# Feed-forward stage: another order of the additions that free banks, of the weight low parts, and another point at which a weight buffer is given back

## Chip, cores and metric

The kernel runs on one core of one Trainium2 chip. The metric is the device time of one execution, in microseconds (us). Before the change the median of 3 runs is 2047.44 us (2047.1 to 2047.58).

## What is computed

The reference is one step of a two-layer streaming encoder over 512 prompt tokens and 128 sample tokens (640 together), model width 1024. Each layer has an attention or recurrence part, a cross-attention, and then the gated feed-forward part that this change is about:

```python
def conv_ffn(h, prev, w_gate, w_up, conv_w, conv_b, w_down):
    g = h @ w_gate                                   # 1024 x 2816
    gp = jnp.concatenate([prev.astype(g.dtype), g], axis=1)
    c = conv_b
    for j in range(CONV_W):                          # 3 taps along the tokens
        c = c + conv_w[j] * gp[:, j:j + t]
    y = (jax.nn.gelu(c) * (h @ w_up)) @ w_down       # 2816 x 1024
    return y, gp[:, t:]
```

All of it is float32. The kernel reaches that accuracy by writing each operand as a high and a low part and taking three products: high by high, high by low, low by high.

## The kernel before, in words

**The stage.** `FFN_PLAN` (L117) lists the chunks of one layer: gate/up chunks `gu 0` to `gu 10`, each of 256 columns of gate and of up, and down chunks `dn 0` to `dn 5`. The order is gu 0, gu 1, dn 0; gu 2, gu 3, dn 1; gu 4, gu 5, dn 2; gu 6, gu 7, dn 3; gu 8, gu 9, gu 10, dn 4, dn 5. In this text a *pair* is one of the six groups gu 2/3, gu 4/5 and gu 6/7 of the two layers with their dn; the *triple* is gu 8/9/10; the *entry* is gu 0, gu 1, dn 0. In the trace, layer 0 has its stage from 602.8 to 1046 us and layer 1 from 1584.9 us to the end.

**A gate/up chunk** is multiplied with seven products in place of eight (a Strassen-like scheme). Its parts are `A11, A12, S1, S2, S3, S4, A22` (L122); each part takes one unit of split weights and gives two results, g and u, of 320 tokens. On TensorE, `gate_up` (L1440) runs 7 x 2 x 12 matmuls. Each result opens the next of 5 PSUM banks (`lin`, class `Banks`), and opening a bank waits until the result that is five places earlier has been drained. So the 14 results form a ring: S1 u waits for the drain of A11 g, S2 u for that of A12 g, S3 g for A12 u, S3 u for S1 g, S4 g for S1 u, A22 u for S3 g, the next chunk's A11 u for S4 g, its A12 g for S4 u, its A12 u for A22 g, its S1 g for A22 u. A *slot* below is one such result, 12 matmuls.

**Who drains.** ScalarE copies A11 (`first_product`). VectorE does the rest: `c11` (A12, and with it the first block of results), `to_sums` (S2 and S1), `c22` (S3), `c12` (S4), `c21` (A22). `taps`, `gated` and `low_a` on VectorE and `tap0`, `gelu` and `high_a` on ScalarE compute the convolution, the gate and the two parts of the activations of the previous chunk.

**Weights.** SyncE loads raw weights into two buffers of 1 MB each (`raw`, L532 to L560); load q waits until the buffer of load q-2 is given back (L542). A gate/up chunk has two loads: the first holds what A11, S2 and S3 come from, the second A12, A22 and S4. GpSimd brings two sums by adding DMAs (`weight_sum`, L743): S1 in tile `sumN`, and S3 in the first raw buffer, after that load has landed. VectorE makes the other two in place: `third_sum` (L2336, for S2) and `fourth_sum` (L2340, for S4, which also reads the first buffer). ScalarE writes the high part of a unit (`refill_hi`, L1709 or L1712) as soon as its raw data is there and its slot, one of 5, is free; then VectorE writes the low part (`refill_lo`, L2321 or L2329). TensorE waits for the low part.

**Order.** Every engine runs its instructions in the order of the program; the order is written out by hand in the loops over `FFN_PLAN` (ScalarE L2110, VectorE L2913). In these loops `f` is the first of the two column blocks of the chunk before, when that was a gate/up chunk; so the second chunk of a pair carries the convolution of the first on VectorE. `g0+4`, `g0+5`, `g0+6` are the units S3, S4, A22 of the chunk at hand, `g0+7` to `g0+10` the first four units of the next. In `down` (VectorE, L2742) each of ten results of 128 x 512 is added to `x`.

Of the kernel before, what the change touches and what calls it, by code (L numbers as in the profile page):

```python
# [15 lines left out]
ALU = mybir.AluOpType  # L16
# [105 lines left out]
PARTS = ("A11", "A12", "S1", "S2", "S3", "S4", "A22")  # L122
HT = TOK // 2
# [92 lines left out]
def build(nc, io, known):  # L216
# [8 lines left out]
    with ctx:  # L225
# [276 lines left out]
        @block.sync  # L502
        def _(sp):
            sp.dma_start(x[:, 0, :], io["x_prompt"][0:P, :]).then_inc(*x_in[0].mark(0))
            sp.dma_start(gain_row[:, :], io["ln_mix"][0:1, :]).then_inc(*gain_in.mark("mix0"))
            sp.dma_start(ident[:, :], io["c_ident"]).then_inc(*ident_in.mark(0))

            def load_x(t):
                src = io["x_prompt"][P * t:P * t + P, :] if t < TP else io["x_sample"]
                sp.dma_start(x[:, t, :], src).then_inc(*x_in[t].mark(t))  # L510

            def gains(nm):

                i = NORMS.index(nm)
                if i:
                    sp.wait_ge(*xn_made.at(NORMS[i - 1], norm_tiles(NORMS[i - 1]) - 1))
                if nm == "cross0":

                    sp.wait_ge(*put["st0"].at(H - 1))
                if nm == "cross1":  # L520

                    sp.wait_ge(*dve_done.at("kz1"))
                if nm in ("mix1", "final"):

                    sp.wait_ge(*dve_done.at("sum", ("gu", 0 if nm == "mix1" else 1, FT // 2 - 1), "S2"))
                src = io["ln_final"] if nm == "final" else io[f"ln_{nm[:-1]}"][int(nm[-1]):int(nm[-1]) + 1]
                sp.dma_start(gain[:, :], src.to_broadcast([P, D])).then_inc(*gain_in.mark(nm))

            before = {("out0", 0): "cross0", ("cq", 0, 1): "mem0", ("co", 0, 0): "ffn0",
                      ("dn", 0, GROUPS - 1): "mix1", ("out1", 1): "cross1", ("cq", 1, 1): "mem1", ("co", 1, 0): "ffn1",  # L530
                      ("dn", 1, GROUPS - 1): "final"}
            for q, (c, u, n) in enumerate(LOADS):  # L532
                if u == 0 and c in before:
                    gains(before[c])
                if q == 1:
                    load_x(1)
                if q == 2:
                    for t in range(2, T):
                        load_x(t)
                if q >= 2:  # L540
                    oc, ou, on = LOADS[q - 2]
                    sp.wait_ge(*lo_made.at(oc, PARTS.index("A22" if ou else "S4") if oc[0] == "gu" else ou + on - 1))  # L542
                s = w_in[q % 2]
                if q == 0:

                    for v in range(n):
                        (src, c0, width), = w_source(c, u + v, 1)
                        dst = raw[:, 0, UNIT * v:UNIT * v + UNIT].rearrange("p (k n) -> p k n", n=512)
                        sp.dma_start(dst, src).then_inc(*(s.mark(q) if v == n - 1 else w_first.mark(0)))
                    continue  # L550
                if c[0] == "ca":
                    sp.dma_start(raw[:, q % 2, 0:P].rearrange("p (k n) -> p k n", k=KT),
                                 io["w_in_odd"][:, 3072:3088].rearrange("(k p) n -> p k n", p=P),
                                 ).then_inc(*s.mark(q))
                    continue
                parts = w_source(c, u, n)
                for i, (src, c0, width) in enumerate(parts):
                    per = 1024 if c[0] == "dn" else 512
                    dst = raw[:, q % 2, 0:n * UNIT].rearrange("p (k n) -> p k n", n=per)[:, :, c0:c0 + width]
                    sp.dma_start(dst, src).then_inc(*(s.mark(q) if i == len(parts) - 1 else s.mark(q, i)))  # L560

            for t in range(T):
                dst = io["o_y_p"][P * t:P * t + P, :] if t < TP else io["o_y_s"]
                src = xn[:, NORM_TILE[("final", t)] % 2, :]
                if t < T - 1:
                    sp.wait_ge(*xn_made.at("final", t))
                    sp.dma_start(dst, src).then_inc(*put[f"y{t % 2}"].mark(t))
                else:
                    for n in range(2):
                        sp.wait_ge(*xn_made.at("final", t, n))  # L570
                        sp.dma_start(dst[:, 512 * n:512 * n + 512], src[:, 512 * n:512 * n + 512]).then_inc(*put[f"y{t % 2}"].mark(t, n))
# [1107 lines left out]
        def _(act):  # L1679
# [277 lines left out]
            def rest(l):  # L1957
# [135 lines left out]
                def high_t(what, dst, src, n, made):  # L2093
                    act.wait_ge(*made)
                    act.activation(dst, src, ACT.Copy).then_inc(*act_done.mark("t_hi", what, l, n))
# [9 lines left out]
                split_hi(("gu", l, 0), [3])  # L2105
                for n in range(2):
                    high_t("t2", t2[0][:, :, CUT[n]], t2F[:, :, CUT[n]], n, dve_done.at("t2F", l, n))
                high_t("t3", t3[0][:, :, :], t3F[:, :, :], 0, dve_done.at("t3F", l))
                turned(1, ("hi",))
                for n, (kind, i) in enumerate(FFN_PLAN):  # L2110
# [19 lines left out]
                        continue  # L2130
                    if f is not None:
                        gelu(f)
                    refill_hi(g0 + 4)
                    if i:
                        first_product(i, "g")
                    if f is not None:
                        gelu(f + 1)
                    if i:
                        first_product(i, "u")
                    if f is not None:  # L2140
                        high_a(f)
                    refill_hi(g0 + 5)
                    if f is not None:
                        high_a(f + 1)
                    refill_hi(g0 + 6)
                    if i == 0:
                        high_t("n4", n4[0][:, :, :], hF[:, 1, :, 0:HT], 0, dve_done.at("n4F", l))
                    refill_hi(g0 + 7)
                    refill_hi(g0 + 8)
                    refill_hi(g0 + 9)  # L2150
# [149 lines left out]
        def _(dve):  # L2300
# [366 lines left out]
            def rest(l):  # L2667
# [165 lines left out]
                def second_tokens(j, key, part, e, signal):  # L2833
# [6 lines left out]
                    if key == "g":  # L2840
# [3 lines left out]
                        dve.tensor_tensor(prompt, one[:, 0:SEQ - HT], two[:, 0:SEQ - HT], ALU.subtract)  # L2844
                        dve.tensor_tensor(seqs, one[:, SEQ - HT:HT].rearrange("p (b w) -> p b w", b=NB), two[:, SEQ - HT:HT].rearrange("p (b w) -> p b w", b=NB), ALU.subtract).then_inc(*signal)
                    else:
                        dve.tensor_tensor(af[e][:, HT:TOK], one[:, 0:HT], two[:, 0:HT], ALU.subtract).then_inc(*signal)  # L2847

                def c22(j, key):
# [54 lines left out]
                low_t2(0)  # L2904
                low_t2(1)
                dve.tensor_tensor(t3F[:, :, :], hF[:, 1, :, HT:TOK], hF[:, 0, :, HT:TOK], ALU.subtract).then_inc(*dve_done.mark("t3F", l))
                fourth_sum(("gu", l, 0))
                dve.wait_ge(*dve_done.at("t2F", l, 1))
                dve.tensor_tensor(hF[:, 1, :, 0:HT], hF[:, 1, :, 0:HT], t2F[:, :, :], ALU.subtract).then_inc(*dve_done.mark("n4F", l))
                low_t("t3", t3[0][:, :, :], t3[1][:, :, :], t3F[:, :, :], 0)  # L2910
                halves(nm, T - 2)
                halves(nm, T - 1)
                for n, (kind, i) in enumerate(FFN_PLAN):  # L2913
                    c = (kind, l, i)
                    g0 = FIRST_UNIT[c]
                    f = 2 * FFN_PLAN[n - 1][1] if n and FFN_PLAN[n - 1][0] == "gu" else None
                    if f is not None:
                        c21(i_before, "u")
                    if kind == "dn":
                        down(i, f)  # L2920
                        continue
                    if f is not None:
                        taps(f + 1)
                        gated(f)
                    refill_lo(g0 + 4)
                    if f is not None:
                        low_a(f)
                        gated(f + 1)
                    c11(i, "g")
                    c11(i, "u")  # L2930
                    refill_lo(g0 + 5)
                    if f is not None:
                        low_a(f + 1)
                    refill_lo(g0 + 6)
                    to_sums(i, "g")
                    to_sums(i, "u")
                    if i == 0:
                        low_t("n4", n4[0][:, :, :], n4[1][:, :, :], hF[:, 1, :, 0:HT], 0)
                    refill_lo(g0 + 7)
                    c22(i, "g")  # L2940
                    c22(i, "u")
                    refill_lo(g0 + 8)
                    c12(i, "g")
                    refill_lo(g0 + 9)
# [4 lines left out]
                    taps(2 * i)  # L2949
                    c21(i, "g")  # L2950
                    if not down_next:
                        refill_lo(g0 + 10)
                    i_before = i

            rest(0)

# [234 lines left out]
```

## Time and profile before

| | us |
|---|---|
| median of 3 runs | 2047.44 |
| the profiled execution, its own time | 2046.7 |
| its span, first to last instruction | 2044.9 |
| TensorE busy in the span | 1985.2 (97%) |
| VectorE busy | 1246.2 (61%) |
| ScalarE busy | 817.2 (40%) |
| GpSimd busy | 422.6 (21%) |
| mean granted TensorE clock | 0.995 |

TensorE (PE) is the engine that sets the time: what counts is where it waits. Busy time is a union of the matmuls' durations, whose ends are modelled and overlap; the distance from one matmul's start to the next is the better measure of pace. A line of the timeline gives start, duration, engine, source line, what is written and read, and in brackets the idle time of the engine before it and who ended it. DVE is VectorE, ACT ScalarE, POOL GpSimd, SPq the queue of SyncE.

### The profile page before, as it was taken

What the parts mean: (1) busy time and instruction counts of PE and PEld (TensorE: products, weight loads), DVE (VectorE), ACT (ScalarE), POOL (GpSimd) and SP (SyncE); (2) the same over time, 40 slices, a digit from 0 to 9 for tenths busy, and PEclk for the clock granted to TensorE, in tenths of its full rate; (3) what the DMA queues carried; (4) which work ended last, traced back from release to release, by engine and by line L of the source; (5) the groups of instructions that cost most, each with busy time, mean ns of one, the idle gap of its engine ahead of it and who ended that gap; (6) DMA issues with size and microseconds to landing.
All of it is one profiled execution on the core that took longest, in us unless ns stands there. A gap on an engine that the chain in (4) does not pass through costs nothing. (4 is left out here: it accounts for less than half of the span.)

```text
span 2044.9 us, 30005 instructions
## 1 busy us (share of the span) xinstructions
PE 1985.2 (97%) x11870; PEld 1723.1 (84%) x11870; DVE 1246.2 (61%) x2086; ACT 817.2 (40%) x1324; POOL 422.6 (21%) x590
## 2 busy tenths in 40 slices
PE   9999989999998999999999999999999899999998
PEld 7889767997788888989889888799877898988986
DVE  5453664435458867677853467643454977768784
ACT  4222552435354433333443446243534533424342
POOL 3012121000133313223110123210012322313311
PEclk9999999999999999999999999999999999999999
DMA  5324144235735546445321211623484464545441
GB/s 176 126 70 160 52 155 140 93 119 197 271 86 127 112 108 149 104 114 134 104 79 63 83 42 47 229 107 124 153 316 111 97 141 114 134 102 136 93 145 56
DMA packets 161052, 254.01 MB, mean 124 GB/s; under 512 B 9123, under 2 KB 99535, under 8 KB 160846
## 3 DMA queue, kind: packets, MB, share of 16 engines
q1 hardware_dynamic: 91234, 148.00, 21.3%
q0 software_dynamic: 69680, 104.08, 21.1%
q8 instruction: 97, 1.59, 0.3%
q14 instruction: 41, 0.34, 0.1%
HBM read 235.11 MB, written 18.24 MB: 124 GB/s over the span
## 5 line engine op out<-in xcount | busy, mean ns | idle before, releaser
L2329 DVE TENSOR_TENSOR w_lo<-raw,w_hi 128x1024 fp32r<-128x1024 f32 x177 | 212.9, 1217 | 234.4 <-ACT w_hi L1712 230.9
L897 PE MATMUL bank<-w_hi,hT_lo 128*128 128x512 f32 x720 | 290.4, 403 | 1.2 <-DVE hT_lo L2388 0.7
L899 PE MATMUL bank<-w_hi,hT_hi 128*128 128x512 f32 x720 | 281.7, 391 | 0.0
L898 PE MATMUL bank<-w_lo,hT_hi 128*128 128x512 f32 x720 | 281.1, 390 | 0.0
L897 PE MATMUL bank<-hT_hi,w_lo 128*128 128x320 f32 (+2 forms) x800 | 249.6, 312 | 5.4 <-DVE af L2866 4.6
L899 PE MATMUL bank<-hT_hi,w_hi 128*128 128x320 f32 (+2 forms) x800 | 247.5, 309 | 0.0
L898 PE MATMUL bank<-hT_lo,w_hi 128*128 128x320 f32 (+2 forms) x800 | 247.4, 309 | 0.0
L1712 ACT ACTIVATE w_hi<-raw 128x1024 fp32r<-128x1024 f32 x177 | 182.6, 1051 | 151.8 <-DMA raw<-w_ffn_down 76.8
L1709 ACT ACTIVATE w_hi<-raw 128x1024 fp32r<-128x1024 f32 x132 | 137.1, 1053 | 257.2 <-DMA raw<-w_ffn_up 132.1
L2321 DVE TENSOR_TENSOR w_lo<-raw,w_hi 128x1024 fp32r<-128x1024 f32 x132 | 160.0, 1218 | 68.5 <-ACT w_hi L1709 68.4
L2402 DVE TENSOR_TENSOR x<-x,bank 128x512 f32<-128x512 f32 x160 | 109.5, 684 | 131.0 <-PE bank L899 130.5
L897 PEld LDWEIGHTS bank<-w_hi,hT_lo 128*128 128x128 f32 x720 | 135.5, 188 | 40.5 <-issue 10.3
L897 PE MATMUL bank<-w_hi,a_lo 128*128 128x512 f32 x400 | 158.9, 397 | 9.2 <-DVE w_lo L2329 7.3
L899 PEld LDWEIGHTS bank<-w_hi,hT_hi 128*128 128x128 f32 x720 | 135.4, 188 | 29.3
L897 PEld LDWEIGHTS bank<-hT_hi,w_lo 128*128 128x128 f32 x800 | 150.5, 188 | 9.8 <-issue 7.9
L898 PEld LDWEIGHTS bank<-w_lo,hT_hi 128*128 128x128 f32 x720 | 135.7, 189 | 25.2
L899 PE MATMUL bank<-w_hi,a_hi 128*128 128x512 f32 x400 | 156.2, 390 | 0.0
L898 PE MATMUL bank<-w_lo,a_hi 128*128 128x512 f32 x400 | 156.1, 390 | 0.0
L898 PEld LDWEIGHTS bank<-hT_lo,w_hi 128*128 128x128 f32 x800 | 150.5, 188 | 0.5
L899 PEld LDWEIGHTS bank<-hT_hi,w_hi 128*128 128x128 f32 x800 | 150.4, 188 | 0.0
L897 PE MATMUL bank<-t_hi,w_lo 128*128 128x320 f32 x352 | 113.3, 322 | 18.1 <-DVE gp L2823 11.7
L898 PE MATMUL bank<-t_lo,w_hi 128*128 128x320 f32 x352 | 110.4, 314 | 0.0
(440 smaller groups left out, 4158.7 us busy)
## 6 DMA issues: line engine op xcount, KB each, us to landing
raw<-w_ffn_gate SPq DMA_DIRECT2D x44, 512.0 KB, 5.2
raw<-w_ffn_up SPq DMA_DIRECT2D x44, 512.0 KB, 7.0
raw<-w_ffn_down SPq DMA_DIRECT2D x22, 1024.0 KB, 6.7
kcX<-cache_mem_k POOLq DMA_DIRECT2D x16, 1024.0 KB, 6.3
vcX<-cache_mem_v POOLq DMA_DIRECT2D x16, 1024.0 KB, 5.9
raw<-w_in_even SPq DMA_DIRECT2D x13, 1024.0 KB, 5.6
raw<-w_in_odd SPq DMA_DIRECT2D x12, 1024.0 KB, 5.1
sumN<-w_ffn_gate POOLq DMA_DIRECT2D x40, 256.0 KB, 4.1
```

Source lines behind the costliest of these rows:

```text
L897: pe.matmul(out, wl, xh, start=first, stop=False)
L898: pe.matmul(out, wh, xl, start=False, stop=False)
L899: return pe.matmul(out, wh, xh, start=False, stop=last)
L1709: act.activation(w_hi[:, g % W_SLOTS, :].rearrange("p (q n) -> p q n", n=P), part_source(c, u), ACT.Copy).then_inc(*hi_made.mark(c, u))
L1712: act.activation(w_hi[:, g % W_SLOTS, 0:n], raw[:, q % 2, UNIT * i:UNIT * i + n], ACT.Copy).then_inc(*hi_made.mark(c, u))
L2321: dve.tensor_tensor(lo, part_source(c, u), flat(hi), ALU.subtract).then_inc(*lo_made.mark(c, u))
L2329: dve.tensor_tensor(w_lo[:, s, 0:n], raw[:, q % 2, UNIT * i:UNIT * i + n], flat(w_hi[:, s, 0:n]), ALU.subtract).then_inc(*lo_made.mark(c, u))
L2402: ins = dve.tensor_tensor(xs, xs, lin.bank(c, t, *key)[:, :], ALU.add)
```

## The change

It reorders instructions and moves two waits; no arithmetic, no transfer and no buffer is added or taken away.

- SyncE: the first raw buffer of a gate/up chunk is given back when the fourth sum is made and the low part of S3 is done, where it was given back after the low part of S4. The second buffer is given back after the low part of A22, as before.
- VectorE, all chunks: `to_sums` comes before the low part of A22 (`g0+6`); `c22` comes before the next chunk's first low part (`g0+7`); `c21(i, "u")` comes before the low part of the next chunk's S2 (`g0+10`) when a gate/up chunk follows.
- VectorE, second chunks: `c11` comes before `taps(f+1)`; `gated(f+1)` and `low_a(f+1)` come after `to_sums` and the low part of A22.
- VectorE, gu 0: `c11` and the low part of S3 come right after t3F is made, ahead of t3's low part and of the fourth sum; the operand of A22 (n4F) is made between the two `to_sums`.
- ScalarE follows this order; in gu 0 the high part of S3 comes ahead of t3's high part.
- One wait of VectorE on its own earlier result is added (`second_tokens`).

```diff
@@ sync @@
-                    sp.wait_ge(*lo_made.at(oc, PARTS.index("A22" if ou else "S4") if oc[0] == "gu" else ou + on - 1))
+                    if oc[0] == "gu" and ou == 0:
+                        sp.wait_ge(*dve_done.at("sum", oc, "S4"))
+                        sp.wait_ge(*lo_made.at(oc, PARTS.index("S3")))
+                    else:
+                        sp.wait_ge(*lo_made.at(oc, PARTS.index("A22") if oc[0] == "gu" else ou + on - 1))
@@ scalar @@
+                refill_hi(FIRST_UNIT[("gu", l, 0)] + 4)
                 high_t("t3", t3[0][:, :, :], t3F[:, :, :], 0, dve_done.at("t3F", l))
...
                     if f is not None:
                         gelu(f)
-                    refill_hi(g0 + 4)
                     if i:
+                        refill_hi(g0 + 4)
                         first_product(i, "g")
                     if f is not None:
-                        gelu(f + 1)
+                        high_a(f)
                     if i:
                         first_product(i, "u")
-                    if f is not None:
-                        high_a(f)
                     refill_hi(g0 + 5)
                     if f is not None:
-                        high_a(f + 1)
-                    refill_hi(g0 + 6)
+                        gelu(f + 1)
                     if i == 0:
                         high_t("n4", n4[0][:, :, :], hF[:, 1, :, 0:HT], 0, dve_done.at("n4F", l))
+                    refill_hi(g0 + 6)
+                    if f is not None:
+                        high_a(f + 1)
@@ vector @@
                     else:
+                        if f >= 2:
+                            dve.wait_ge(*dve_done.at("a", l, f - 2))
...
                 dve.tensor_tensor(t3F[:, :, :], hF[:, 1, :, HT:TOK], hF[:, 0, :, HT:TOK], ALU.subtract).then_inc(*dve_done.mark("t3F", l))
+                c11(0, "g")
+                c11(0, "u")
+                refill_lo(FIRST_UNIT[("gu", l, 0)] + 4)
+                low_t("t3", t3[0][:, :, :], t3[1][:, :, :], t3F[:, :, :], 0)
                 fourth_sum(("gu", l, 0))
-                dve.wait_ge(*dve_done.at("t2F", l, 1))
-                dve.tensor_tensor(hF[:, 1, :, 0:HT], hF[:, 1, :, 0:HT], t2F[:, :, :], ALU.subtract).then_inc(*dve_done.mark("n4F", l))
-                low_t("t3", t3[0][:, :, :], t3[1][:, :, :], t3F[:, :, :], 0)
...
                     if f is not None:
-                        taps(f + 1)
                         gated(f)
-                    refill_lo(g0 + 4)
+                    if i:
+                        refill_lo(g0 + 4)
                     if f is not None:
                         low_a(f)
+                    if i:
+                        c11(i, "g")
+                        c11(i, "u")
+                    if f is not None:
+                        taps(f + 1)
+                    refill_lo(g0 + 5)
+                    to_sums(i, "g")
+                    if i == 0:
+                        dve.wait_ge(*dve_done.at("t2F", l, 1))
+                        dve.tensor_tensor(hF[:, 1, :, 0:HT], hF[:, 1, :, 0:HT], t2F[:, :, :], ALU.subtract).then_inc(*dve_done.mark("n4F", l))
+                    to_sums(i, "u")
+                    refill_lo(g0 + 6)
+                    if f is not None:
                         gated(f + 1)
-                    c11(i, "g")
-                    c11(i, "u")
-                    refill_lo(g0 + 5)
-                    if f is not None:
                         low_a(f + 1)
-                    refill_lo(g0 + 6)
-                    to_sums(i, "g")
-                    to_sums(i, "u")
                     if i == 0:
                         low_t("n4", n4[0][:, :, :], n4[1][:, :, :], hF[:, 1, :, 0:HT], 0)
-                    refill_lo(g0 + 7)
                     c22(i, "g")
                     c22(i, "u")
+                    refill_lo(g0 + 7)
                     refill_lo(g0 + 8)
                     c12(i, "g")
                     refill_lo(g0 + 9)
...
                     c21(i, "g")
                     if not down_next:
+                        c21(i, "u")
                         refill_lo(g0 + 10)
```

## Rows read from the trace of the kernel before

**Rows 1.** The page: busy time of TensorE, its share, its matmuls.
```profile
PE 1985.2 (97%) x11870; PEld 1723.1 (84%) x11870; DVE 1246.2 (61%) x2086; ACT 817.2 (40%) x1324; POOL 422.6 (21%) x590
```

**Rows 2.** Waits of TensorE: us in total, times, longest.
```profile
PE bank L897 <- DVE gp L2823: 11.7, 2, 5.9
PE bank L897 <- DVE w_lo L2329: 7.3, 6, 1.2
PE bank L897 <- DVE p1g L2831: 5.7, 11, 0.5
PE bank L897 <- DVE af L2866: 4.6, 7, 0.7
...
PE bank L897 <- DVE u2g L2852: 3.4, 7, 0.8
```

**Rows 3.** Timeline of gu 0, layer 0: start, duration, engine, what, [idle before].
```profile
615.18 1.48 DVE L2906 TENSOR_TENSOR t3F<-hF 128x1280 f32<-128x1280 f32 x1
...
623.38 0.64 PE L897 MATMUL bank<-t_hi,w_lo 128*128 128x320 f32 x1 [5.84 <-DVE gp L2823]
...
623.65 2.35 DVE L2321 TENSOR_TENSOR w_lo<-raw,w_hi 128x1024 fp32r<-128x1024 f32 x2
```

**Rows 4.** Timeline of TensorE in gu 7: pace, and the wait of S1.
```profile
873.88 0.31 PE L899 MATMUL bank<-hT_hi,w_hi 128*128 128x320 f32 x1
...
874.32 0.31 PE L899 MATMUL bank<-hT_hi,w_hi 128*128 128x320 f32 x1
875.36 0.39 PE L897 MATMUL bank<-hT_hi,w_lo 128*128 128x320 f32 x1 [0.73 <-DVE af L2866]
```

**Rows 5.** Timeline of VectorE and SyncE in gu 6, a first chunk.
```profile
849.59 1.21 DVE L2321 TENSOR_TENSOR w_lo<-raw,w_hi 128x1024 fp32r<-128x1024 f32 x1
...
851.52 2.35 DVE L2321 TENSOR_TENSOR w_lo<-raw,w_hi 128x1024 fp32r<-128x1024 f32 x2
...
853.89 0.68 SPq L560 DMA_DIRECT2D raw<-w_ffn_gate  x1
...
857.38 0.49 DVE L2831 TENSOR_TENSOR p1u<-u2u,bank 128x320 f32<-128x320 f32 x1
```

**Rows 6.** Timeline: second load's landing in gu 6, and c21 behind it.
```profile
864.95 1.06 ACT L1709 ACTIVATE w_hi<-raw 128x1024 fp32r<-128x1024 f32 x1 [3.13 <-DMA raw<-w_ffn_up]
...
872.07 0.48 DVE L2866 TENSOR_TENSOR gp<-u2g,bank 128x320 f32<-128x320 f32 x1
```

**Rows 7.** Timeline of gu 7, a second chunk: c21 u, last sum, first down unit.
```profile
874.74 0.48 DVE L2866 TENSOR_TENSOR af<-u2u,bank 128x320 f32<-128x320 f32 x1
...
882.41 2.24 SPq L560 DMA_DIRECT2D raw<-w_ffn_down  x2
...
885.61 0.49 DVE L2831 TENSOR_TENSOR p1u<-u2u,bank 128x320 f32<-128x320 f32 x1
...
888.97 2.01 ACT L1712 ACTIVATE w_hi<-raw 128x1024 fp32r<-128x1024 f32 x2 [6.79 <-DMA raw<-w_ffn_down]
```

**Rows 8.** Timeline: a load by itself (issue; GpSimd's wait for its landing).
```profile
894.10 0.37 SPq L560 DMA_DIRECT2D raw<-w_ffn_gate  x1
...
899.65 1.27 POOL L766 DMA_DIRECT2D raw<-w_ffn_gate  x1 [17.67 <-DMA raw<-w_ffn_up]
```

**Rows 9.** Windows: us, PE busy, others, then granted clock, DMA share, GB/s.
```profile
620.00:627.00 7.00, 3.62 (x13) 3.62 (x14) 6.89 (x11) 2.44 (x3) 0.00 (x0) 0.52 0.11 21
...
268.00:272.00 4.00, 3.40 (x14) 3.26 (x15) 3.40 (x10) 1.54 (x2) 1.64 (x3) 0.58 0.94 356
```

**Rows 10.** Timeline of TensorE: pairs' first matmul and wait for the fourth down unit.
```profile
679.26 0.31 PE L897 MATMUL bank<-hT_hi,w_lo 128*128 128x320 f32 x1
...
734.94 0.50 PE L897 MATMUL bank<-w_hi,a_lo 128*128 128x512 f32 x1 [1.22 <-DVE w_lo L2329]
...
842.58 0.30 PE L897 MATMUL bank<-hT_hi,w_lo 128*128 128x320 f32 x1
...
897.91 0.50 PE L897 MATMUL bank<-w_hi,a_lo 128*128 128x512 f32 x1 [1.22 <-DVE w_lo L2329]
...
1821.72 0.31 PE L897 MATMUL bank<-hT_hi,w_lo 128*128 128x320 f32 x1
...
1876.50 0.51 PE L897 MATMUL bank<-w_hi,a_lo 128*128 128x512 f32 x1 [1.22 <-DVE w_lo L2329]
```

More of the change, by code:

```diff
@@ L2916, in rest @@
                     f = 2 * FFN_PLAN[n - 1][1] if n and FFN_PLAN[n - 1][0] == "gu" else None
-                    if f is not None:
-                        c21(i_before, "u")
                     if kind == "dn":
+                        if f is not None:
+                            c21(f // 2, "u")
                         down(i, f)
@@ L2922, in rest @@
                     if f is not None:
-                        taps(f + 1)
                         gated(f)
-                    refill_lo(g0 + 4)
+                    if i:
+                        refill_lo(g0 + 4)
                     if f is not None:
                         low_a(f)
+                    if i:
[10 more added lines that the diff above has]
+                    refill_lo(g0 + 6)
+                    if f is not None:
                         gated(f + 1)
-                    c11(i, "g")
-                    c11(i, "u")
-                    refill_lo(g0 + 5)
-                    if f is not None:
                         low_a(f + 1)
-                    refill_lo(g0 + 6)
-                    to_sums(i, "g")
-                    to_sums(i, "u")
                     if i == 0:
                         low_t("n4", n4[0][:, :, :], n4[1][:, :, :], hF[:, 1, :, 0:HT], 0)
-                    refill_lo(g0 + 7)
                     c22(i, "g")
                     c22(i, "u")
+                    refill_lo(g0 + 7)
                     refill_lo(g0 + 8)
@@ L2951, in rest @@
                     if not down_next:
+                        c21(i, "u")
                         refill_lo(g0 + 10)
-                    i_before = i
             rest(0)
```

## The prediction

> **What bounds the kernel.** I read the page first: TensorE is busy 97% of the span [rows 1], so a change of order can only win back its idle time, some 60 us, and what a stretch at low clock costs. The waits of TensorE show whose they are [rows 2]: once per layer 5.8 us for the first result block of gu 0 (`c11`, L2823), and some thirty short ones for `to_sums` (L2831), `c21` u (L2866), `c22` (L2852) and the low parts of down units (L2329). All are waits for VectorE in the feed-forward stage and 32.7 us in sum. The timeline then shows why VectorE is late: not by its own sum of work but by its order. In gu 0 it is ready with t3F at 616.7, yet does `c11` only behind the fourth sum, n4F, t3's low part and others, and TensorE stands until 623.4 [rows 3]; the stretch 620 to 627 shows a mean granted clock of 0.52, the 1.2 GHz level [rows 9]. In second chunks `c21` u stands behind a low part and the fourth sum, `to_sums` behind the low part of A22, `c22` behind the next chunk's first low part, which waits for a load.
>
> **Units of the sum.** Matmuls of 320 columns start 0.147 us apart (two distances make 873.88 to 874.32 [rows 4]), so a slot is 12 x 0.147 = 1.76 us. I measure a pair from its first matmul to the matmul that waits for the fourth down unit: 55.7 us in the first, 55.3 in gu 6/7, 54.8 in the last [rows 10]. The other three, read the same way, are 57.1, 56.6 and 54.7; all six together 334.2. With no wait it would be 28 slots and nine matmuls of 0.227 (the down matmuls' distance), 51.4.
>
> **Step 1, the second load leaves later.** In a first chunk VectorE now makes A22's low part behind both `to_sums`. The last of these ends at 857.9 in gu 6 and stays there, since it waits for TensorE's S2 u; with the low part's 1.2 the buffer is back at 859.05, 16.5 us after the chunk's start at 842.6, where it was 11.3 (853.9) [rows 5]. The first load, in turn, leaves after S3's low part (850.8, +8.3) instead of after S4's (852.7, half of the 2.35).
>
> **Step 2, but it lands sooner after it left.** Before, the two loads and the adding DMA of S1 ran at once, and the second landed 11.0 us after its issue (853.89 to 864.95, where ScalarE's wait ends [rows 5, 6]). A load by itself takes 5.5 (894.10 to 899.65 [rows 8]). Now the first load has 8 us to itself and the S1 sum; the second meets the adding DMA of S3. A down load that met an adding DMA and the start of another load took 6.5 (882.41 to 888.97 [rows 7]). I take 6.8, nearest to this row, as an estimate between 5.5 and 11.0. So landing is at L = 16.5 + 6.8 = 23.3 after the chunk's start, where it was 22.4. The Trainium skill (DMA: Bandwidth & Descriptors, Issuing engines are not separate DMA queues) says that DMAs of all issuers interleave on the same 16 engines; the 11.0 beside the 5.5 agrees. Its section Anatomy of one DMA gives 2.0 us and bytes over 436 GB/s, an estimate of 4.4 us for 1 MB; by that L would be 20.9 and the time that of the second rival below, but the row for one load is 5.5.
>
> **Step 3, from L to A12 u.** Low part of A12, `c12` g, low part of S1, third sum, `c12` u, taps, `c21` g follow L one by one; `c21` g ends 7.6 after L in gu 6 (864.95 to 872.55 [rows 6]) and nothing in this piece is reordered. A12 u of the second chunk would be due at 17 slots, 29.9, and comes at 23.3 + 7.7 = 31.0: TensorE still waits, 1.1 us per pair, spread over A12 g and A12 u. In return `c21` u is done 0.4 later rather than 2.7, so the wait of S1 (0.73 idle [rows 4]) goes.
>
> **Step 4, from A12 u to the fourth down unit.** From `c21` u to the last `to_sums` VectorE works without a pause for 11.4 us (874.74 to 886.10 [rows 7]); then it waited until 890.06 for a down unit. The same instructions are there after the change, with the low part of S2 and the fourth sum (2.3) now behind `c21` u and `gated`, `low_a` at the end, which wait 0.85 for ScalarE's high part. Then come, with no DMA to wait for, `c22` twice (1.7), two low parts (2.3) and `c12` g (0.5). From `c21` u at L + 7.5: 7.5 + 11.4 + 2.3 + 0.85 + 1.7 + 2.3 + 0.5 = 26.5. Behind `c12` g stand `tap0`, the fourth unit's high part and its low part, 3.4 us (before: 894.5 to 897.91). The second down load leaves at L + 19.6 and lands about 6 later (5.5 to 7.2), and the third unit's high part (1.05) delays `tap0` by 0.2. So the matmul comes at L + 30.1 = 53.4. `to_sums` g ends 0.5 before S3 u is due and `c22` 1.9 before A22 u, so the waits for L2831 and L2852 go. Six pairs: 334.2 - 6 x 53.4 = 13.8 us won.
>
> **Step 5, the triple.** gu 8 to gu 9 goes as above. In gu 9 the second load for gu 10 leaves at L + 19.8 and meets two adding DMAs; I take 7.2, landing at 23.3 + 27 = 50.3, and the fourth down unit at 80.4 after gu 8's start. Before it was 81.3 in layer 0 and 79.7 in layer 1: 0.2 won.
>
> **Step 6, the entry.** `c11` at 616.6 frees S2 u at once, which takes away the 5.8. What is late next: t3's low part (620.0; S3 g waits 1.0), then `to_sums` g, which stands behind the fourth sum, two low parts of activations and S4's low part, until 624.4 (S3 u waits 2.6), then S4 g 0.6. gu 1 begins at 634.4 instead of 637.4. But A22's low part is now made at 629.4 instead of 626.0 (second of the two in [rows 3]), behind `to_sums` and n4F; the second load of gu 1 lands at about 636.0 (before 633.4), and `c12` g behind it holds A11 u until 638.8, then 1.5 more before A12 u at 643.7 (before 642.7). ScalarE's first Gelu brings a table load, and S1 u waits another 1.0. At the sixth down result I get 68.1 after gu 0's start; before 68.5 in layer 0 and 67.1 in layer 1. So the largest wait of all is turned into waits for a load: 0.4 won, 1.0 lost. The clock: at 268 a gap of 2.3 us was followed by a stretch of 0.58 [rows 9], and the entry has two gaps of 2.6; as most of what is slowed there waits anyway, I count 0.5 per layer lost. Together -1.6. The Trainium skill (TensorE: Matmul & The Clock Gate, Loop structure matters more than you think) says that idle TensorE falls to half clock; rows 9 agree for 5.8 us of idle time. By that rule alone removing the gap would give back about 2 us per layer (13 to 17 matmuls 0.12 longer); my sum has that inside, since it goes from start to start.
>
> **Edits at nothing.** The first load's earlier return: it is hidden, since the first load is no longer what anyone waits for; if it stood alone it would cost nothing either. `gelu(f+1)` and `taps(f+1)` later: GpSimd's `halo` and with it the adding DMA of S1 is queued behind them and leaves some 3 us later, which is what meets the second down load in step 4; S1 itself has over 10 us left. ScalarE's `first_product` g now comes 0.5 before its bank is due. The added wait is for a result long made: at 0 to 0.05 each, 20 times, under 1 us. TensorE's, SyncE's and GpSimd's order is unchanged, and no queue is passed.
>
> **Sum.** 13.8 + 0.2 - 1.6 = 12.4 us off the profiled execution's 2046.7, which is 0.7 below the median of the runs. On the median: 2047.4 - 12.4 = 2035.0.
>
> **The rivals.** Everything hangs on the time T from the second load's issue to its landing: one us more costs 6 in the pairs, about 4 in the triples (it enters twice) and 2 in the entries.
> (a) Forecast, T from 5.8 to 7.5: 2023 to 2043. For it: the loads that met one adding DMA. Chance 0.62.
> (b) T of 5.5 or less, and the pairs come near TensorE's own 51.4: pairs 21, triples 5, entries 1, so 2020. For it: 5.5 for a load by itself; against: the adding DMA is always there. Chance 0.07.
> (c) The waits only change their names: T of 7.5 to 8.2; at 8, L = 24.5, pairs +6.6, triples -4.6, entries -4, 2 us slower, 2049. For it: the row of 11.0 has two transfers beside it, and half of its excess over 5.5 would give 8.2. That the change doesn't do what it says belongs here: the 0.5 us that `to_sums` and `first_product` have in hand are gone if one more wait of ScalarE is on the way. Chance 0.17.
> (d) Slower: the second load, given back 5.2 us later, meets the S3 sum head on and takes 9 us or more, as 11.0 before. It decides from T = 8.2, where the pairs' gain is eaten by the triples, in which the delay enters twice. At T = 9 pairs 0.6, triples -8.6, entries -6: 14 slower, 2061; at 11 some 2085. Against it: in the row of 11.0 three transfers ran, here two. Chance 0.14.
>
> **How the numbers follow.** The time is that of (a), 2035.0. Its own range is 2023 to 2043. To leave out no more than 2 in 10 I leave out (d) nearly whole and the lower part of (b), and take in most of (c): 2022 to 2048. A measurement of this kernel can tell 0.2%, 4.1 us, from no change. Faster by more: (a) nearly whole and (b), 0.68; within: (c) and the rim of (a), 0.18; slower: (d), 0.14.
>
> **What would show it.** Right: no wait of 5.8 us behind L2823; L2831 and L2852 nearly gone from TensorE's waits; new waits for `c12` (L2847, L2845) and `c21` at A11 u to A12 u; in gu 6 the second load leaves 16.5 after the start and lands at 22.5 to 24; in pairs 52.5 to 54.5 us. Wrong at step 2, if that landing is off; at step 4, if the waits of L2329 at the fourth down unit grow though the loads are there; at step 6, if gu 1's A12 u is not 1 us later than before. The prediction falls as a whole if SyncE's second load leaves at another time than 16.5.

## The result: slower, and the profile after

The changed kernel takes 2056.76 us (median of 5 runs, 2054.36 to 2064.16), the kernel before 2047.58 beside it (2047.1 to 2049.22). The ratio is 1.0050 (95% interval 1.0034 to 1.0067): **slower by half a per cent**, outside the range, where 2035.0 was predicted. The profiled execution took 2056.31 us with a span of 2054.5, which is 9.6 more than the span of before.

Waits of TensorE in the changed kernel, in us, with their number and the longest; they answer to [rows 2]:

```profile
PE bank L901 <- DVE gp L2850: 19.6, 11, 3.4
PE bank L901 <- DVE af L2854: 6.6, 10, 0.7
PE bank L901 <- DVE w_lo L2334: 6.3, 9, 0.8
PE bank L901 <- DVE p1g L2836: 4.7, 2, 2.4
```

The wait for the first result block (11.7) is gone, and so are those for `to_sums` in second chunks, `c21` u and `c22`; what is left of L2836 is `to_sums` in gu 0, 2.4 in each layer. A new one has come, larger than all of them: L2850, `c12` g, at the A11 u of second chunks, in 11 of the 12. In the kernel before the same addition is L2845, and it stands in no row of [rows 2]. Where the time went, chunk by chunk, from first matmul to first matmul (us; a pair here runs to the start of the next chunk, the triple ends with gu 10's last matmul, the entry runs from gu 0 to gu 2):

| | before | changed | predicted gain | measured gain |
|---|---|---|---|---|
| six pairs | 485.9 | 483.0 | 13.8 | 2.9 |
| two triples | 156.4 | 163.5 | 0.2 | -7.1 |
| two entries | 151.6 | 156.9 | -1.6 | -5.3 |
| sum | | | 12.4 | -9.5 |

Counted by the distance from one matmul's start to the next, beyond 0.147 us (0.227 in down chunks), the entries have 4.0 us more of waits than before and 1.3 more of matmuls that follow one another slowly without a wait; the triples have 3.9 and 3.2 more.

The timeline of the changed kernel in gu 6 and the start of gu 7 (start, duration, engine, what, idle before), the piece of [rows 5, 6]. gu 6 starts at 842.2:

```profile
850.46 0.37 SPq L564 DMA_DIRECT2D raw<-w_ffn_gate  x1
...
856.26 1.27 POOL L770 DMA_DIRECT2D raw<-w_ffn_gate  x1 [3.10 <-DMA raw<-w_ffn_up]
...
858.61 0.37 SPq L564 DMA_DIRECT2D raw<-w_ffn_gate  x1
...
867.00 1.06 ACT L1713 ACTIVATE w_hi<-raw 128x1024 fp32r<-128x1024 f32 x1 [9.94 <-DMA raw<-w_ffn_up]
...
869.84 0.42 PE L901 MATMUL bank<-hT_hi,w_lo 128*128 128x320 f32 x1 [1.16 <-DVE gp L2850]
```

The second load leaves at +16.45, as predicted (858.61). It needs 8.4 us and not 6.8 (ScalarE's wait for it ends at 867.00), since GpSimd has sent S3's adding DMA 2.4 us ahead of it (0.8 to 2.4 ahead in the eight first chunks). The row at 856.26 also says what GpSimd had waited for: the landing of the first load. I did not draw the consequence of that: **the load that the change lets go 2 us earlier is what releases the adding DMA**.

### The profile page after: what moved, and what is told of

Its sections match the earlier page's. It is cut to its first block and busy times, and to the rows that moved or that the text cites. A ratio compares the mean times of both kernels' runs of the same rounds, so it can differ in the third digit from the quotient of the medians.

```text
span 2054.5 us, 30027 instructions
## 1 busy us (share of the span) xinstructions
PE 1987.5 (97%) x11870; PEld 1726.3 (84%) x11870; DVE 1247.4 (61%) x2086; ACT 816.1 (40%) x1324; POOL 411.9 (20%) x590
## 5 line engine op out<-in xcount | busy, mean ns | idle before, releaser
L901 PE MATMUL bank<-hT_hi,w_lo 128*128 128x320 f32 (+2 forms) x800 | 254.9, 319 | 27.1 <-DVE gp L2850 19.6
```

The lines of the kernel that those rows point to most:

```text
L901: pe.matmul(out, wl, xh, start=first, stop=False)
```

## The experiments

Eleven kernels. Each was timed beside the kernel before on the same chip; the table has the ratio to it with its 95% interval. "Pairs", "triples" and "entries" are the sums of the table above from the profiled execution. Then come, as means over the eight first chunks of pairs and triples (gu 2, 4, 6 and 8 of both layers), when the second load leaves after the chunk's start, its time T from issue to landing, and the landing L after the start; the landing is read where ScalarE's wait for the load ends.

| kernel | us | ratio | pairs | triples | entries | out | T | L |
|---|---|---|---|---|---|---|---|---|
| before | | 1 | 485.9 | 156.4 | 151.6 | 11.7 | 10.2 | 22.0 |
| changed | 2056.8 | 1.0050 (1.0034-1.0067) | 483.0 | 163.5 | 156.9 | 16.5 | 8.2 | 24.7 |
| s3_held | 2025.0 | 0.9884 (0.9870-0.9899) | 469.5 | 151.0 | 152.9 | 16.5 | 5.6 | 22.0 |
| rest_only | 2050.4 | 1.0018 (1.0007-1.0029) | 482.7 | 156.5 | 157.2 | 16.5 | 5.9 | 22.4 |
| changed_second | 2036.8 | 0.9947 (0.9932-0.9962) | 470.7 | 156.5 | 156.3 | 16.5 | 5.9 | 22.4 |
| a22_early | 2033.7 | 0.9927 (0.9912-0.9942) | 465.1 | 156.2 | 157.2 | 11.7 | 9.5 | 21.1 |
| entry_old | 2047.3 | 0.9997 (0.9986-1.0009) | 484.1 | 161.8 | 146.8 | 16.5 | 8.3 | 24.8 |
| release_alone | 2012.9 | 0.9833 (0.9817-0.9850) | 462.1 | 151.3 | 146.2 | 11.3 | 9.2 | 20.5 |
| release_second | 2027.2 | 0.9902 (0.9887-0.9917) | 470.8 | 157.1 | 146.6 | 11.5 | 10.5 | 22.0 |
| release_s3_held | 2008.4 | 0.9818 (0.9802-0.9834) | 461.1 | 149.8 | 146.7 | 11.1 | 9.0 | 20.0 |
| a22_all_entry_old | 2021.2 | 0.9881 (0.9864-0.9898) | 467.2 | 153.2 | 147.2 | 11.6 | 9.4 | 21.0 |
| a22_all_entry_mended | 2021.4 | 0.9883 (0.9864-0.9902) | 467.8 | 152.8 | 146.8 | 11.7 | 9.4 | 21.0 |
| banks_first_hi_load | 2011.2 | 0.9822 (0.9806-0.9839) | 461.9 | 150.5 | 146.7 | 11.5 | 8.9 | 20.4 |

### Is the second load late, and what makes it so?

**s3_held** makes S3's adding DMA wait for the second load too, in every chunk but gu 0:

```diff
 elif part == "S3":
     pool.wait_ge(*w_in[q0 % 2].at(q0))
+    if j:
+        pool.wait_ge(*w_in[(q0 + 1) % 2].at(q0 + 1))
```

> The changed kernel, but GpSimd issues the adding DMA of S3 only after the second load has landed, so that the second load never meets it. Theory 1 in its strong form (the collision is what makes the landing slow): from issue to landing 5.5 to 5.8 us instead of 7.4 to 9.5, the wait at A11 u nearly gone, pairs 52 to 53 us instead of 54 to 56, in all 2028 to 2038 us. Rival (the load is slow for another reason, the S1 sum or HBM): landing time stays above 7 and the time within 4 us of 2056.8.

Measured 2025.0. Its timeline in gu 6, which starts at 832.4:

```profile
848.90 0.37 SPq L564 DMA_DIRECT2D raw<-w_ffn_gate  x1
...
854.96 1.06 ACT L1715 ACTIVATE w_hi<-raw 128x1024 fp32r<-128x1024 f32 x1 [7.51 <-DMA raw<-w_ffn_up]
...
855.48 1.27 POOL L772 DMA_DIRECT2D raw<-w_ffn_gate  x1 [11.94 <-DMA raw<-w_ffn_up]
```

The load leaves at the same +16.5 and takes 6.1 us, since the adding DMA goes only when it has landed. This alone takes the wait for `c12` g from 19.6 to 2.4 and the time 32 us below the changed kernel's: 13.5 in the pairs, 12.5 in the triples, 4.0 in the entries. The gain is larger than I had put down. T is 2.6 us shorter in the mean, and the prediction's own price, 12 us for each us of T, makes 31 of it. The waits for low parts of down units do not go with it: they are 9.1 here and 6.3 in the changed kernel.

**a22_early** moves A22's low part ahead of both `to_sums` again, in first chunks:

```diff
 refill_lo(g0 + 5)
+early = i and f is None
+if early:
+    refill_lo(g0 + 6)
 to_sums(i, "g")
...
 to_sums(i, "u")
-refill_lo(g0 + 6)
+if not early:
+    refill_lo(g0 + 6)
```

> The changed kernel, but in the first chunks of the pairs and triples A22's low part is made ahead of both to_sums, where it stood before. Theory 1 (the second load leaves 5.2 us later than before and meets the adding DMA of S3, so it lands late): the second load leaves at +11.3 of the chunk instead of +16.5 and lands by +20 to +21 instead of +23.8 to +25.9; the waits at A11 u, A12 g and A12 u of second chunks go, 2 to 3.5 us for each of eight places, so about 2032 to 2038 us. Theory 2 (VectorE's new order in the second chunks or the entry is what costs, not the load): within 4 us of the changed kernel's 2056.8.

Measured 2033.7, as expected. T is long again (9.5), but the load leaves 4.8 us sooner. What counts is L: with 21.1 no second chunk of a pair waits at A11 u.

**rest_only** and **changed_second** turn to the SyncE hunk. The first leaves it out (the buffer goes back at S4's low part, as before); the second keeps it in second chunks only:

```diff
 if oc[0] == "gu" and ou == 0:
-    sp.wait_ge(*dve_done.at("sum", oc, "S4"))
-    sp.wait_ge(*lo_made.at(oc, PARTS.index("S3")))
+    if oc[2] in (1, 3, 5, 7, 10):
+        sp.wait_ge(*dve_done.at("sum", oc, "S4"))
+        sp.wait_ge(*lo_made.at(oc, PARTS.index("S3")))
+    else:
+        sp.wait_ge(*lo_made.at(oc, PARTS.index("S4")))
```

> The changed kernel with the old wait on SyncE (the first raw buffer is again given back at S4's low part); all the reorderings stay. Theory 1 (the hunk is worth what the chain it feeds is short of: in the new order the second load leaves at +16.45 of a first chunk whatever the first one does, and only 1.9 us of the first load and 4.3 us of the down load move): 1 to 2 us a pair and as much in a triple, so 2063 to 2072. Rival (the hunk is worth the same 35 us in any order, because the down loads and the first loads always leave late without it): 2088 to 2095. Rival 2 (the hunk is what put the loads among the adding DMAs here, so that it costs in this order): 2045 to 2054.

> The changed kernel with the earlier return in the second chunks alone; in first chunks the buffer goes back at S4's low part as before. Theory (in the new order the hunk sends S3's adding DMA out ahead of the second load, since that DMA leaves when the first load has landed; in rest_only it left behind, and the second load took 5.9 us and not 8.2. The down loads gain from the hunk): the second load takes 5.3 to 6.7 us and the waits at A11u after a first chunk are gone, the waits for w_lo in the down projections are those of the changed kernel, 1.3 us a pair and not 2.4, so 2040 to 2046, below both rest_only (2050) and the changed kernel (2057). Rival (the adding DMA is not what makes the second load long, the down loads of the chunk before are): second load over 7 us, 2052 or more.

Measured 2050.4 and 2036.8. The first fell on the rival by which the hunk costs something in this order; the second was faster than expected. The timeline of changed_second in gu 6, which starts at 838.3:

```profile
848.44 0.37 SPq L567 DMA_DIRECT2D raw<-w_ffn_gate  x1
...
854.71 0.37 SPq L567 DMA_DIRECT2D raw<-w_ffn_gate  x1
...
856.43 1.27 POOL L773 DMA_DIRECT2D raw<-w_ffn_gate  x1 [6.98 <-DMA raw<-w_ffn_up]
...
860.65 1.06 ACT L1716 ACTIVATE w_hi<-raw 128x1024 fp32r<-128x1024 f32 x1 [3.42 <-DMA raw<-w_ffn_up]
```

The first load leaves 1.9 us later than in the changed kernel (+10.2), lands later, and releases the adding DMA 1.7 us behind the second load and not 2.4 ahead of it (1.7 to 3.7 behind in the eight chunks). The second load then takes 5.9. So the hunk in first chunks, which gives a load away sooner, costs the changed kernel 1.0050 - 0.9947, about 21 us. That is shown from two sides: by a later first load here, by a held adding DMA in s3_held.

rest_only shows what is late next. Its waits, and rows of gu 3 and of the down projection behind it; the first holds the issues of both down loads, the second the landing of the second of them:

```profile
PE bank L897 <- DVE w_lo L2330: 13.6, 13, 2.2
```

```profile
720.78 3.35 SPq L560 DMA_DIRECT2D raw<-w_ffn_down  x2
...
731.90 1.06 ACT L1712 ACTIVATE w_hi<-raw 128x1024 fp32r<-128x1024 f32 x1 [3.66 <-DMA raw<-w_ffn_down]
...
734.27 0.50 PE L897 MATMUL bank<-w_hi,a_lo 128*128 128x512 f32 x1 [1.51 <-DVE w_lo L2330]
...
736.05 0.50 PE L897 MATMUL bank<-w_hi,a_lo 128*128 128x512 f32 x1 [0.81 <-DVE w_lo L2330]
```

The low parts of down units had 7.3 us of waits in [rows 2] and have 13.6, for the third and the fourth unit. The buffer of the second down load is given back by A22's low part in the second chunk. That load leaves 16.9 to 18.2 us after the second chunk's start and takes 7.7 to 9.0, so that it lands at 25.6 in the mean (25.0 before), while the down projection now begins 1 to 3 us sooner. In changed_second it leaves at the same point, but the first down load has gone some 4.5 us earlier, and it takes 6.3 to 8.0; the waits for low parts are 7.9 there.

### The hunk that "would cost nothing alone"

**release_alone** is the kernel before with the SyncE hunk and nothing else. **release_second** restricts it to second chunks, with the `oc[2]` test above. **release_s3_held** is release_alone with the wait of s3_held.

> The kernel before with one hunk of the change, the earlier return of the first raw buffer. The prediction said it costs and gives nothing by itself: 2047.5 within 1.5. Rival: the first load leaves 2 us earlier, the second then has less of it beside itself and lands up to 1 us earlier, which shortens the waits at S1 and A12 u of second chunks: 2043 to 2045.

> The kernel before with the earlier return of the first raw buffer in the second chunks alone (gu1, 3, 5, 7 and 10); in the others it waits for S4's low part as before. Theory (the 35 us of release_alone have two halves: in first chunks the first load leaves 2 us earlier and the second lands 1.5 us earlier, which ends the bank waits of the second chunk, 2.3 to 3.5 us a pair; in second chunks the down load leaves 5 us earlier, which ends the waits of 1.4 to 1.9 us in the down projections): the second half alone, 1.5 to 2.5 us a pair and 1 to 2 us an entry, so 2031 to 2038. Rival (the down load is the head of the whole chain and carries all of it): 2012 to 2020. Rival 2 (it all comes from the first chunks): 2044 to 2048.

> release_alone with S3's adding DMA held until the second load has landed. Theory 1 (the meeting of the two costs 1.5 to 3 us of landing time, and a landing costs the kernel only where something waits for it; in release_alone the second load has 4 us to spare): second load lands some 1.5 us earlier and nothing follows, 2011 to 2015. Rival (the meeting costs wherever it is, as in s3_held, where holding won 32 us): 2000 to 2008. Rival 2 (the held DMA is now late for S3 of the next chunk): 2016 to 2025.

Measured 2012.9: **one wait given up earlier, by itself, wins 1.67%, some 34 us**. I had put nothing on it. Its waits, then its timeline from gu 6 (start 828.4) to the down load in gu 7 (start 853.0):

```profile
PE bank L901 <- DVE gp L2827: 11.7, 2, 5.9
...
PE bank L901 <- DVE p1g L2835: 3.0, 6, 0.5
PE bank L901 <- DVE w_lo L2333: 1.3, 1, 1.3
```

```profile
836.68 0.37 SPq L564 DMA_DIRECT2D raw<-w_ffn_gate  x1
...
839.70 0.37 SPq L564 DMA_DIRECT2D raw<-w_ffn_gate  x1
...
848.44 1.06 ACT L1713 ACTIVATE w_hi<-raw 128x1024 fp32r<-128x1024 f32 x1 [5.05 <-DMA raw<-w_ffn_up]
...
862.47 5.67 SPq L564 DMA_DIRECT2D raw<-w_ffn_down  x2
```

Two things move. In the first chunk the first load leaves 1.9 us sooner (+8.3) and the second where it did (+11.3); no longer so close behind one another, the second takes 8.7 and lands at +20.0 in gu 6 (848.44) where it was +22.4. In the second chunk the down load leaves at +9.5 (862.47) where [rows 7] have it 15.2 after gu 7's start (882.41 - 867.2). After that most of the small waits of [rows 2] are gone: those for `c21` u and `c22` but for 0.5, those for the low parts of down units (the 1.3 above is at 15 us, outside the stage), and half of those for `to_sums`. Nothing of VectorE's order was touched. What went had been waits for a load, handed down VectorE's queue.

release_second, at 2027.2, has the second half alone: 1.0%, 20 us, more than expected (2031 to 2038). It ends the waits for the low parts, but `to_sums` keeps 5.4 and `c21` u 4.8: these hang on the first chunk's second load. The first half is then 0.9902 - 0.9833, 14 us. release_s3_held was expected to change nothing and gives 0.9818 beside 0.9833, intervals overlapping: holding the DMA that brought 32 us in the new order brings nothing that can be told here. One reason given for it ahead was wrong: the hold was to take 1.5 to 3 us off T, and it takes 0.2 (9.2 to 9.0), though the adding DMA leaves 9 to 11 us behind the second load and not 3 to 4. Where the second load follows the first by 3 us and S1's adding DMA by 2 to 3, it is not S3's that makes it long.

### The entry, and a better kernel

**entry_old** is the changed kernel with gu 0 in the order of before. **a22_all_entry_old** has A22's low part early in second chunks too. **a22_all_entry_mended** has it early everywhere, with the new entry: in gu 0 `to_sums` goes ahead of the fourth sum, and ScalarE makes A22's high part ahead of n4's.

> The changed kernel with gu 0 in the order of before on VectorE and ScalarE (c11 late, A22's low part ahead of to_sums). By the traces the entry, from gu 0 to gu 2, takes 78.8 and 78.0 us after the change and 76.5 and 75.0 before, so if the entry is a part by itself: 5 us less than the changed kernel, 2051 to 2052, with the 5.8 us wait behind L2828 back. Rival (the entry's loss comes from gu 1, which keeps its new order): entry stays at 78, 2056 to 2057.

> The changed kernel with gu0 in the order of before and with A22's low part ahead of both sets of bank-freeing additions in every other chunk (a22_early had that in the first chunks alone). Theory 1 (two losses beside the entry, both made by the late low part of A22: second loads that leave late in first chunks, and down loads that leave late in second chunks, which the waits for low parts in the down projections show): the waits in the down projections go too, 2011 to 2018, level with release_alone. Rival (what a22_early still lacked against release_alone comes from the order of the gelu, low_a and c11 steps, not from the loads): 2022 to 2026.

> The changed kernel with A22's low part early in every chunk, gu0 included; in gu0 the bank-freeing additions also go ahead of the fourth sum, and ScalarE makes A22's high part ahead of n4's. Theory 1 (the changed entry is lost through its second load, which waits for A22's low part, and with that early its gain on TensorE in gu0 is kept): gu0 and gu1 together 56 us or less where release_alone has 59.1, the rest as release_alone, 2004 to 2010. Rival (what is won in gu0 is given back at gu1's A11u as in the changed kernel, since VectorE has no more time there): 2013 to 2018.

entry_old: 2047.3, so the new entry costs some 10 us in the changed kernel and not 5 (entries 156.9 against 146.8). The rows of the new one, layer 0:

```profile
627.93 1.23 DVE L2326 TENSOR_TENSOR w_lo<-raw,w_hi 128x1024 fp32r<-128x1024 f32 x1 [1.37 <-ACT w_hi L1713]
...
629.18 0.37 SPq L564 DMA_DIRECT2D raw<-w_ffn_gate  x1
...
639.49 0.41 PE L901 MATMUL bank<-hT_hi,w_lo 128*128 128x320 f32 x1 [3.36 <-DVE gp L2850]
```

A22's low part ends at 629.2, the load lands at 636.6, A11 u of gu 1 starts at 639.5. The earlier start of gu 1 (634.2, before 637.4) is lost in one wait.

a22_all_entry_old: 2021.2, between the two expectations; its waits for low parts of down units are 3.0, where the changed kernel has 6.3 and a22_early 4.5, so the first theory holds for them in part. What it still lacks against release_alone (8 us) is 5.1 in the pairs, 1.9 in the triples and 1.0 in the entries. Waits for the fourth down unit, for `to_sums` of up to 1.0 and in gu 10 are part of it; it was not taken apart further. a22_all_entry_mended ties with it, 2021.4; its gu 0 trades the wait at S3 u for 1.7 at S4 g and 1.8 at A22 g. Not the 2004 to 2010 expected.

**banks_first_hi_load** is release_s3_held with, in gu 0 alone, `c11` ahead of the fourth sum and `to_sums` among the low parts; A22's low part comes 2 us later than there:

```diff
+c11(0, "g")
+c11(0, "u")
 fourth_sum(("gu", l, 0))
...
+to_sums(0, "g")
 refill_lo(g0 + 5)
+to_sums(0, "u")
 refill_lo(g0 + 6)
```

> release_s3_held with two pieces of the change's entry: in gu0 the additions that free the first banks go ahead of the fourth sum, and the additions for S3's bank ahead of the low part that is made beside them; A22's low part and every other chunk stay as they are there. Theory (what the changed entry wins on TensorE is real, and it was given back only because A22's low part moved behind and the second load with it): S2u no longer waits 6 us, gu1 starts some 3 us earlier in each layer, its A11u waits less than 1 us, 2001 to 2005. Rival (VectorE has no time left there, and what is moved ahead is paid by A22 or by gu1's A11u): 2007 to 2010.

Measured 2011.2, ratio 0.9822 beside 0.9818: nothing won. The wait of 5.9 before S2 u comes back as 4.5 before the next matmul group, S3 g:

```profile
623.01 0.64 PE L903 MATMUL bank<-t_hi,w_lo 128*128 128x320 f32 x1 [4.51 <-DVE w_lo L2327]
```

gu 1 begins 1.7 to 1.8 us sooner in each layer, and that is lost again before gu 2. Both rearrangements of gu 0 gave 146.7 to 146.8 for the entries, the old order with the hunk 146.2 to 147.2: what is moved ahead on VectorE is paid behind it. That no order of this work does better isn't shown.

**The best version** is release_alone, with or without the held DMA: 2012.9 and 2008.4, 1.7 to 1.8% below the kernel before.

## Why the prediction was wrong, point by point

**Step 1, held.** The second load leaves at +16.45 in all eight first chunks, the first at +8.3 in gu 6. So the sign by which the prediction was to "fall as a whole", another time than 16.5, did not come.

**Step 2, failed, and with it the sum.** I took T as 6.8 from a down load that met an adding DMA. It is 8.2 in the mean (7.4 to 9.5), 1.4 more, and the landing is at 24.7 and not at 23.3. At the prediction's own price of 12 us for each us of T, this term alone is 16.8 of the 21.8 us between 2035.0 and 2056.8. The sign that it gave for an error here came: in gu 6 the load lands at 24.8, and 22.5 to 24 was to be right. "The second meets the adding DMA of S3" was right. But I never placed that DMA in time. Its release stood in [rows 8], where GpSimd's adding DMA goes when a load of SyncE has landed, and placing it gives 8.3 + 5.5 = +13.8, some 2.5 us ahead of the second load, so that nearly all of it lies beside it. My row 6.5 was the wrong neighbour. The estimate of 4.4 us beside it was no help either: the Trainium skill (DMA: Bandwidth & Descriptors, Anatomy of one DMA) gives that fit for transfers on GpSimd's path, and this load is SyncE's; with the adding DMA held it took 5.3 to 6.1.

**Edits at nothing, failed.** "The first load's earlier return ... would cost nothing either" was wrong by 34 us alone, and with the other sign by 21 in the changed order's first chunks. I asked who waits for this load, and not who waits for the buffer behind it: SyncE's next issue, and GpSimd's.

**Steps 3 and 4, held, but for half a us a pair.** A12 u comes 7.65 us after the landing in every first chunk of a pair, 7.7 predicted; the fourth down unit 30.2 to 31.2 after it, 30.1 predicted, with second down loads of 6.4 to 7.4 us where I had put about 6. On the prediction's own measure the six pairs are 331.3 and not 320.4; the longer T adds up to 8.2 of the missing 10.9. With T at 5.9, at the good end of the forecast, the pairs should have won 19 us (13.8 + 6 x 0.9). changed_second has that T and the hunk in second chunks, as the sum assumed, and wins 15.2. rest_only has that T without the hunk and wins 7.9 on the prediction's measure, and only 3.2 from chunk to chunk, since matmuls are slow behind its two waits. What bounds both is the second down load. I had costed it as "about 6 later" and let nothing hang on it.

**Step 5, failed by T.** The second loads of gu 9 took 9.5 and 9.3 us, 7.2 assumed: in layer 0 both adding DMAs leave at 963.84 and 965.38, the load at 966.85. The four second loads of the triples took 7.5 us more than assumed in sum, and the triples are 7.4 too long on the prediction's measure.

**Step 6, right in its order, too small.** gu 1 starts at 634.2 (634.4 predicted); the wait at A11 u comes and ends 0.7 later than said, A12 u starts 1.2 later, and the sixth down result comes at 70.9 and 70.1, 68.1 predicted. The second load of gu 1 takes 7.5 us where the step has 6.6. The clock term was about right here: slow matmuls cost the two entries 1.3 us more than before, 1.0 assumed. The waits were mis-sized, 4.0 more than before where the step comes to 0.6. What the sum has no clock term for is the triples, where slow matmuls are 3.2 of the 7.1 lost. Windows of the changed kernel (us, PE busy, others, granted clock, DMA share, GB/s), first behind the wait of gu 1, then in gu 10, with the matmul that opens the slow stretch there:

```profile
637.00:644.00 7.00, 4.34 (x19) 3.97 (x20) 6.22 (x9) 3.65 (x4) 2.26 (x2) 0.76 0.01 2
...
979.23 0.64 PE L901 MATMUL bank<-hT_hi,w_lo 128*128 128x320 f32 x1 [3.00 <-DVE gp L2850]
...
980.00:983.00 3.00, 3.00 (x13) 3.00 (x12) 2.96 (x5) 1.34 (x2) 1.50 (x2) 0.50 0.00 0
983.00:990.00 7.00, 7.00 (x42) 7.00 (x41) 7.00 (x11) 4.86 (x7) 1.53 (x3) 0.83 0.12 12
```

In gu 10, behind 3.0 us of idle time that end at 979.23, 21 matmuls start 0.267 us apart and not 0.147, so that this chunk, whose A11 u is 3.2 us late, is 6.1 us longer than its 14 slots. The Trainium skill (TensorE: Matmul & The Clock Gate, Loop structure matters more than you think) says that an idle TensorE falls to half clock, and the 0.50 here agrees. How much of it would have been waits for VectorE at full clock is not shown.

**The rivals.** What happened lies where (c) ends and (d) begins, by (d)'s mechanism: the second load meets the S3 sum head on. T is 8.2 in first chunks, (d)'s deciding point, not the 9 it names, and 9.4 in gu 9, where it "enters twice"; the triples lost most. I gave (d) 0.14 because "here two" transfers ran and not three; but the row of 11.0 had S3's adding DMA beside it as well in its last 3.9 us (861.02 to 864.95), and two that overlap nearly wholly are enough. The range reached only to T = 7.9: at 8.2 the prediction's own prices give 2051.8. The other 5 us, up to 2056.8, are the pairs' half us each, the longer T of gu 9 and the waits of the entries.

## What to carry to other kernels

When a buffer goes back at another time, follow it to every issuer that waits on its landing, and write the new order of all transfers on one time axis before taking a duration for any; the same early return won 14 us in one order and lost 21 in the other. A row of waits names the last hand in a chain: many small waits for different additions on one engine can be one or two late loads, and the cheap test is to send the load earlier and leave the engine's order alone. Change one thing at a time: the hunk alone beats the whole change by over 2%.

## What the runs showed of the hardware

- A load of 1 MB takes 5.3 to 6.5 us from issue to landing when S3's adding DMA is sent 1.7 to 3.7 us behind it (changed_second), 7.4 to 9.5 when it is sent 0.8 to 2.4 ahead (changed), and 9.7 to 11.1 when another load leaves 1.1 to 1.8 us and S1's adding DMA 2.5 to 3.2 us ahead of it (before). Going first does not help the adding DMA: from its first issue to its last landing it takes 7.9 to 11.4 us in the changed kernel and 6.5 to 7.7 in changed_second. The Trainium skill (DMA: Bandwidth & Descriptors, Issuing engines are not separate DMA queues) says that the issuers share the 16 engines; that fits, but the order of issue changes what both transfers take. Why is not shown.
- The price of TensorE's idle time is not even. In the changed kernel a first matmul of A11 u that came 2.4 us late (gu 5 of layer 1) was followed by matmuls at full pace, one 2.8 us late (gu 1 of layer 1) by ten at 0.267 us, one 3.2 us late (gu 10 of layer 0) by 21. Two waits close together did it too: behind the 1.51 and 0.81 us of idle time above, eight down matmuls of rest_only are 0.43 us apart and not 0.23, 1.7 us more.
